# Both rest-decay products of the SSM preparation on GpSimd, none on VectorE

## The reference

```python
dstate = jnp.exp(acum[..., -1:] - acum)
states = jnp.einsum('bclgn,bcgrl,bclgrp->bcgrpn', bc, dstate, xc)
y_diag = jnp.einsum('bcgls,bcgrls,bcsgrp->bclgrp', cb, lmat, xc)
...
y_off = jnp.einsum('blgn,bgrpn,bgrl->blgrp', c_i, S, din_i)
S = S * cd_i[..., None, None] + st_i
```

## Time and profile before

| | us |
|---|---|
| median of 3 runs (lowest, highest) | 3794.55 (3783.8, 3806.95) |
| the profiled execution, its time | 3795.41 |
| its span on the core | 3793.7 |
| TensorE busy | 3617.4 (95%) |
| VectorE busy | 1944.5 (51%) |
| ScalarE busy | 1149.6 (30%) |
| GpSimd busy | 686.1 (18%) |

### The profile page before, as it was taken

How to read it: one execution, slowest core, us unless ns; L and a number is a source line. 1 busy time by engine, 2 the same in 40 slices (tenths; PEclk the granted TensorE clock), 3 DMA queues, 4 the chain that set the end, 5 groups by cost and what they waited for, 6 DMA issues and landing times.

```text
span 3793.7 us, 66122 instructions
## 1 busy us (share of the span) xinstructions
PE 3617.4 (95%) x27915; PEld 3406.9 (90%) x27915; DVE 1944.5 (51%) x2337; ACT 1149.6 (30%) x1970; POOL 686.1 (18%) x733
## 2 busy tenths in 40 slices
PE   7999999999899898999999999999998998889998
PEld 6999999999888766899989999999997887488998
DVE  6531454233456686685375224533325667856753
ACT  4211121122366552331122101112224666342311
POOL 1110111122410352100011101112234005511000
PEclk9999999999999999999999999999998999999999
DMA  6333223333621397752333232322336215876422
GB/s 247 111 108 93 88 84 92 95 127 104 247 78 35 127 326 254 228 170 72 106 120 102 88 107 87 94 87 92 127 110 238 59 36 175 278 243 190 141 78 108
DMA packets 364136, 507.54 MB, mean 134 GB/s; under 512 B 83168, under 2 KB 287816, under 8 KB 360912
## 3 DMA queue, kind: packets, MB, share of 16 engines
q1 hardware_dynamic: 311096, 375.81, 30.6%
q0 software_dynamic: 36768, 103.68, 9.1%
q10 hardware_dynamic: 16000, 24.12, 1.9%
HBM read 331.21 MB, written 172.32 MB: 133 GB/s over the span
## 4 chain that ended last, share of the span: by engine, by line
PE 80%; DVE 6%; DMA 3%; issue 3%; DVEq 2%; SPq 2%; ACT 1%; POOL 1%; POOLq 0%; ACTq 0%
PE PSUM L858 10%; PE PSUM L860 10%; PE PSUM L859 10%; PE PSUM L1416 4%; PE PSUM L1418 4%; PE PSUM L1417 4%; PE PSUM L1691 4%; PE PSUM L1530 3%; PE PSUM L1823 3%; PE PSUM L1825 3%; PE PSUM L1517 3%; PE PSUM L1824 3%; PE PSUM L1496 2%; PE PSUM L1890 2%; PE PSUM L1891 2%
## 5 line engine op out<-in xcount | busy, mean ns | idle before, releaser
L858 PE MATMUL PSUM<-h_hi,w_hi 128*128 128x384 f32 x2304 | 771.4, 335 | 4.8 <-DVEq L2788 2.1
L860 PE MATMUL PSUM<-h_hi,w_lo 128*128 128x384 f32 x2304 | 769.8, 334 | 0.0
L859 PE MATMUL PSUM<-h_lo,w_hi 128*128 128x384 f32 x2304 | 769.7, 334 | 0.0
L858 PEld LDWEIGHTS PSUM<-h_hi,w_hi 128*128 128x128 f32 x2304 | 432.5, 188 | 9.7 <-issue 9.6
L859 PEld LDWEIGHTS PSUM<-h_lo,w_hi 128*128 128x128 f32 x2304 | 432.5, 188 | 0.0
L860 PEld LDWEIGHTS PSUM<-h_hi,w_lo 128*128 128x128 f32 x2304 | 432.5, 188 | 0.0
L2418 POOL DMA_DIRECT2D proj_d<-leave x140 | 131.8, 942 | 1377.1 <-DVE leave L2784 543.6
L1416 PE MATMUL PSUM<-h_hi,w_hi 128*128 128x384 f32 x960 | 325.1, 339 | 0.0
L1417 PE MATMUL PSUM<-h_lo,w_hi 128*128 128x384 f32 x960 | 321.3, 335 | 0.0
L1418 PE MATMUL PSUM<-h_hi,w_lo 128*128 128x384 f32 x960 | 321.2, 335 | 0.0
L2890 DVE TENSOR_REDUCE row_max<-PSUM 128x1 f32<-128x1152 f32 x128 | 173.7, 1357 | 158.2 <-PE PSUM L1497 157.9
(11 more groups left out here) (428 smaller groups left out, 7214.8 us busy)
## 6 DMA issues: line engine op xcount, KB each, us to landing
proj_d<-leave POOLq DMA_DIRECT2D x140, 512.0 KB, 3.9
w_raw<-in_w_in SPq DMA_DIRECT2D x54, 1024.0 KB, 5.6
gdn_tile_d<-g_out SPq DMA_DIRECT2D x18, 1536.0 KB, 7.9
wide_br<-proj_d SPq DMA_DIRECT2D x48, 576.0 KB, 4.3
xs<-ssm_tok_d SPq DMA_DIRECT2D x32, 640.0 KB, 7.7
ssm_tok_d<-x_rest SPq DMA_DIRECT2D x36, 512.0 KB, 3.6
w_in<-in_w_in SPq DMA_DIRECT2D x16, 1024.0 KB, 6.2
av_t<-gdn_tile_d SPq DMA_DIRECT2D x28, 512.0 KB, 5.9
```

Source lines behind the costliest of these rows:

```text
L858: pe.matmul(dst, wh, x_hi[:, k, lo:hi], start=(k == 0), stop=False)
L859: pe.matmul(dst, wh, x_lo[:, k, lo:hi], start=False, stop=False)
L860: last = pe.matmul(dst, wl, x_hi[:, k, lo:hi], start=False, stop=(k == kt - 1))
```

## The change

The forward product moves from VectorE's list, where it was the last instruction of tile t, to GpSimd's, right ahead of the backward product of the same tile. It signals the same semaphore `sp_xr`, so SyncE's waits are unchanged.

```diff
@@ GpSimd, preparation, tile t
                     if t == 0:
                         pool.wait_ge(xy_stored, l * 160 + 160)
                         pool.sem_inc(waits_held, 1)
+                    pool.tensor_tensor(x_rest[p][0][:], xt[p][:, 0:D_MODEL].rearrange("p (h q) -> p h q", q=SP_), over(dt_rest[:, 0, t], SP_), ALU.mult).then_inc(sp_xr, 1)
                     pool.tensor_tensor(x_rest[p][1][:], xt[p][:, 0:D_MODEL].rearrange("p (h q) -> p h q", q=SP_), over(dt_rest[:, 1, t], SP_), ALU.mult).then_inc(pool_made, 1)
@@ VectorE, preparation, tile t
                             if t == 0:
                                 dve.wait_ge(xy_stored, l * 160 + 160)
                             dve.tensor_tensor(d_x[p][:, 8:SH], xt[p][:, 8 * SP_:D_MODEL].rearrange("p (h q) -> p h q", q=SP_), over(rows[:, 88:96], SP_), ALU.mult)
-                            dve.tensor_tensor(x_rest[p][0][:], xt[p][:, 0:D_MODEL].rearrange("p (h q) -> p h q", q=SP_), over(dt_rest[:, 0, t], SP_), ALU.mult).then_inc(sp_xr, 1)
```

## The result

The changed kernel has a median of 3812.95 us over 11 runs (3809.28 to 3822.53); the kernel before, run beside it on the same chip, has 3798.27 us over 11 (3783.8 to 3807.88). The ratio is 1.0043, with a 95% interval from 1.0033 to 1.0054: slower by 12.5 to 20.5 us. That is certain, and still inside the 0.5% within which the prediction called it the same. The profiled execution has a span of 3810.4 us, 16.7 more than before.

A forecast was written before the change was run, and what follows sets the result against it. It took a loop through TensorE, ScalarE, GpSimd and VectorE to bound layer 1, and TensorE's own loop layer 0. Terms 6.6 + 0.1 + 4.2 + 0.7 + 0.1 = +11.7 us gave 3806.3 on 3794.55, range 3789 to 3820.

The forecast's parts named there:

- step b: Steady tiles: GpSimd's second product holds e_ssm's sum; period 10.24 us, +6.6 in layer 1, +4.2 in layer 0.
- (a): Both layers: 18 VectorE products of 1.22 us go, hidden behind TensorE in steady tiles: 0.
- The tails: Behind tile 8: layer 1 sets 1.32 late against a 1.22 product gone, +0.1; layer 0, TensorE had room, +0.1.
- Starts: First tiles: layer 0 +0.7 from tile 2; layer 1 taken as 0, bounds -3 and +1, GpSimd handing back the gain.
- the queues: SP's stores and GpSimd's loads for tile t+2: loads start about 1 us later, wanted over a period later; both 0.
- the second price: GpSimd's product at the skill's estimated 2.25 us: pair 4.5 us, period 11.0, sum about +21.
- The first (no new wait): Steady tiles: VectorE wins each time, GpSimd's second product slips behind w_ssm; -6.8, 3788 us; chance 0.11.
- the second (VectorE is the bound): Both layers: the removed VectorE product was on the path; 18 x 1.22 = -22, 3773 us; chance 0.03.
- The third: DMA issues behind GpSimd's pair also slow e_ssm's sum and w_ssm, 0.9 us a tile; +12 more, 3818; chance 0.12.

The follow-up runs named there:

- x_memset: Changed kernel, but GpSimd makes two memsets of zeros behind the backward product in place of the forward product; ratio 1.0007 to the kernel before.
- x_oneinput: Changed kernel, but GpSimd multiplies one SBUF input by a constant behind the backward product, in place of the forward product; ratio 1.0028 to the kernel before.
- x_none: Changed kernel with the forward product made by no engine, only a one-column memset for the signal; ratio 0.9995 to the kernel before.
- x_from3: Changed kernel, but tiles 0 to 2 keep the forward product on VectorE, the others have it on GpSimd; ratio 1.0039 to the kernel before.
- x_third: Changed kernel with the forward product made twice on GpSimd, so three products a tile; ratio 1.0162 to the kernel before.
- x_vector: Changed kernel, but with both products on VectorE and none on GpSimd; ratio 1.0001 to the kernel before.
- x_place: Changed kernel, but GpSimd's forward product stands behind the backward one and waits for w_ssm of half 0; ratio 1.0044 to the kernel before.
- x_place2: As x_place, but GpSimd's backward product also waits for VectorE's copy of cb, behind d_x; ratio 1.0029 to the kernel before.

## Why the prediction was right, and where it was not

Where two measured numbers stand, they are the first profiles of both kernels compared, and then the second ones.

**The loop (step b)** held to the hundredth: 10.24 us forecast, 10.23 to 10.25 measured in both layers, its legs as worked out. x_memset and x_oneinput show that the hold is the cause, since the period of steady tiles shortens as the hold does. Tiles 3 to 8 of layer 0: forecast +4.2, measured +4.2 and +4.5. Of layer 1: forecast +6.6, measured +8.0 and +6.6.

**The products that VectorE loses (a)** were put at nothing in steady tiles, and that was right: 18 of them gone, and x_none still gains only 4 us, of which 1.4 is layer 1's tail, the one that step (b) set against the last hold. The tails rose by 0.1 to 0.2, forecast +0.1.

**Starts.** Layer 0, forecast +0.7, measured -1.8 and +0.5, from profiles that differ by 2.2 among themselves, so little can be said of it. From tile 2 to tile 3 alone it is 12.03 against 11.37 in the first pair, the +0.7, and 12.00 against 12.03 in the second. Layer 1 is the term that was mis-sized: taken as 0 with bounds of -3 and +1, it measured +2.4 and +2.6. Its first part came as worked out: the transposes of tile 2 start 21.62 us behind those of tile 0 in place of 24.81, 3.2 sooner. The second, that GpSimd hands this back and no more, didn't: tile 2 to tile 3 took 16.46 us in place of 10.91. Start of layer 1 in the changed kernel, VectorE and GpSimd (compare):

```profile
3184.51 2.87 POOL L2535 TENSOR_TENSOR x_rest<-xt,dt_rest 128x1024 f32<-128x1024 f32 x1
3186.04 2.42 DVE L3023 TENSOR_TENSOR w_ssm<-e_ssm,cb 128x1024 f32<-128x1024 f32 x1 [0.43 <-issue]
...
3188.98 2.45 DVE L3021 TENSOR_TENSOR e_ssm<-e_ssm,e_ssm 128x1024 f32<-128x1024 f32 x1
3189.20 2.37 PE L1616 MATMUL PSUM<-cst,xin 128*128 128x128 f32 x10 [4.29 <-DVE y_acc L3003]
...
3190.40 2.79 POOL L2534 TENSOR_TENSOR x_rest<-xt,dt_rest 128x1024 f32<-128x1024 f32 x1
3191.51 2.77 DVE L3023 TENSOR_TENSOR w_ssm<-e_ssm,cb 128x1024 f32<-128x1024 f32 x1
3193.16 2.87 POOL L2535 TENSOR_TENSOR x_rest<-xt,dt_rest 128x1024 f32<-128x1024 f32 x1
3194.20 2.38 DVE L3030 TENSOR_TENSOR d_x<-xt,rows 128x512 f32<-128x512 f32 x1
```

Four operations are held here (w 2.42, e 2.45, w 2.77, d_x 2.38 in place of 1.23, 1.22, 1.23 and 0.69), 5.65 us together; with the sums of 1.99 and 1.78 and a `w_ssm` of 2.77 around them it is 8.5 us over the start, against 4.1 before (2.92, 2.12 and 2.77). The prediction has GpSimd fall behind, but names no hold of VectorE at the start. And TensorE, which waits 4.29 us in the middle of it, comes back at the 1.2 GHz level. Its windows (the granted clock third from the end):

```profile
3185.00:3189.20 4.20, 0.00 (x0) 0.03 (x1) 3.77 (x4) 1.24 (x6) 4.20 (x5) 0.87 1.00 391
3189.20:3197.00 7.80, 5.53 (x20) 4.75 (x21) 7.64 (x4) 1.50 (x3) 7.79 (x7) 0.50 0.74 253
3197.00:3205.60 8.60, 5.69 (x76) 4.10 (x74) 5.84 (x5) 5.82 (x12) 8.59 (x11) 0.90 0.84 293
3205.60:3209.00 3.40, 3.34 (x16) 3.33 (x17) 3.04 (x4) 0.17 (x1) 1.24 (x3) 0.56 0.40 111
```

The ten transposes take 2.37 us at the 1.2 GHz level and 1.28 at the 2.4 GHz one. The kernel before has such a stretch too (0.57 from 3185.0 to 3190.5, behind a wait of 3.64 us); the changed one has a longer one, and in the first profile a second, behind a wait of 2.97 us, in just the period that took 11.64. In the second profile the clock was back for those transposes (1.28 us), and the period was 10.23.

x_from3 shows that the products of the first three tiles cost the +2.4. The timelines say how it adds up. TensorE's first exponent of tile 2, in the changed kernel and then in the kernel before:

```profile
3194.69 0.79 PE L1607 MATMUL PSUM<-far_r,ident_r 128*128 128x512 f32 x1 [2.27 <-DMA s_col<-steprow_d]
...
3187.89 0.77 PE L1607 MATMUL PSUM<-far_r,ident_r 128*128 128x512 f32 x1
```

It waits for the decay rows of tile 2, whose loads GpSimd issues behind both products of tile 0: 19.7 us behind the transposes of tile 0 in place of 17.1 (19.9 and 17.0 in the second profiles, with a wait of 2.73). So these exponents begin 27.1 and 27.7 us behind the transposes of tile 0, as before (27.7 and 27.6), and the 3.2 us are gone. The prediction had put the queues at 0, because the loads "are wanted more than a period later"; at this start they are wanted at once. From these exponents to the transposes of tile 3 it is 10.97 in place of 8.05 us, and 10.81 in place of 8.32. TensorE's part of that, up to y_acc of half 0, grew by 0.8 and 1.4, with more of it at the 1.2 GHz level; VectorE's part, from y_acc to y_acc, grew by 2.1 and 1.1, which are its held operations. Every run in which GpSimd's list was longer than before in the first tiles has a wait for these loads (x_oneinput 6.00, x_third 5.42, x_memset 5.36); x_vector, x_from3 and both profiles of before have none. x_none has one too (2.73), with its loads issued as early as before, since tile 2 comes 4.0 us sooner: what VectorE's product held back there, these loads hold back next.

**The sum.** Forecast +11.7 us; the stretches gave +13.0 and +14.4, the difference being layer 1's start and, in the first pair, also its first period (+1.4), against which layer 0's start stands with 2.5 below its forecast. The prediction also let layer 0's stretch begin at 1299 us, but its first transposes are at 1292.99; the two stretches are 197 us, not 191, which changes nothing in the sum. By the medians of 11 runs it is +14.7. The time of 3812.95 lies 7 us above the forecast of 3806, of which 3.7 are the median of before, 3798.27 with more runs in place of 3794.55. The +21 that the second price gave was too much: the Trainium skill (GPSIMD Engine Reference, "Elementwise — side-by-side cycle accounting") leads by estimate to 2.25 us for a product, and the rows have 1.90, twice in a row in each tile.

**Rivals.** The first (no new wait) and the second (VectorE is the bound) are out by the period. The third was right in its phenomenon and wrong in its place. A product behind DMA issues does hold VectorE during them, by 0.9 us and more, but only where it has been released already. In steady tiles of the changed kernel ScalarE's copy comes 3.5 us after GpSimd went idle, so the issues there cost nothing: `w_ssm` at 3235.81 keeps its 1.22 us through three of them. The same mechanism made periods of 10.9 us in x_place, from a placement that looked harmless.

## What to carry to other kernels

Moving an elementwise operation from VectorE to GpSimd took nothing off VectorE's busy time here, because both engines read SBUF at the same moment. So don't ask which engine has time, but which VectorE operation arrives while GpSimd's runs, and whether that one is on the loop. Here 36 products on VectorE gave a shorter steady period in layer 1 (9.27 us) than none (10.24). A late placement of the GpSimd operation only helps if the next one in its queue isn't already released. First measure what the operation is worth by leaving it out altogether: here 4 us of 3797, so moving this one product could hardly pay. It is no floor for a split that moves the other product too: the start of layer 1 is 2.4 us shorter with all products on VectorE (33.10) than with this one left out (35.49). And look at what else stands in the queue that gets the work: loads behind it go out later, which cost nothing in steady tiles and did at the start of a layer.

## What the runs showed of the hardware

- A VectorE operation with both inputs in SBUF is also held while GpSimd only issues DMAs, if a GpSimd product whose waits are met stands behind them: 3.94 us in place of 1.23 in x_memset, 3.20 in place of 0.69 in x_place. With that product not yet released, and the same issues under way, it takes 0.68 us (x_place2, and x_place itself at 3232.74).
- The Trainium skill (SBUF — State Buffer, "SBUF: two separate sides") describes the exclusion between the two engines as a lock for a whole instruction, which a VectorE operation with two SBUF inputs meets only against a GpSimd operation that reads SBUF. The runs agree on both: 2.79 us in place of 1.22 against two SBUF inputs, a hold against one too (period 9.39), none against a MEMSET (1.22). Only the length for one input is open: the hold was about 1.0 us by estimate, from the sum's end at 3232.08 and the 1.08 us, and the profile gives that instruction 2.76.
- When both engines have such work all the time, they alternate operation by operation (x_third, start of layer 1), and each of them is stretched. GpSimd's 1.90 us products then read 2.8 to 2.9 us and VectorE's of 1.22 us 2.4 to 2.8.
